# Matmul order in the projections and gate/up: each product runs over all token chunks in turn

## The reference, cut to what matters

```python
def hybrid_mixer(h, hc, ...):
    aq, ak, av, bq, bk, bv, z, xbc, dt = split_projection(h @ w_in)
    caq, cak, cav, cbq, cbk, cbv, cz, cxbc, cdt = split_projection(hc @ w_in)
    ...
    y = jnp.concatenate([out_a, out_b, out_c], -1) @ w_out

def swiglu(h, w_gu, w_down):
    gate, up = jnp.split(h @ w_gu, 2, axis=-1)
    return (jax.nn.silu(gate) * up) @ w_down
```

## Time and profile before

| what | us |
|---|---|
| median of 3 runs | 3884.65 |
| lowest and highest | 3880.82, 3886.8 |
| profiled execution, first to last instruction (span) | 3878.7 |
| PE busy in it | 3426.3 (88%) |
| DVE, POOL, ACT busy in it | 1871.5, 1411.6, 853.1 |

### The profile page before, as it was taken

How to read it: one execution, slowest core, us unless ns; L and a number is a source line. 1 busy time by engine, 2 the same in 40 slices (tenths; PEclk the granted TensorE clock), 3 DMA queues, 4 the chain that set the end, 5 groups by cost and what they waited for, 6 DMA issues and landing times. The chain is left out here.

```text
span 3878.7 us, 48787 instructions
## 1 busy us (share of the span) xinstructions
PE 3426.3 (88%) x17688; PEld 2858.7 (74%) x17688; DVE 1871.5 (48%) x2851; ACT 853.1 (22%) x1566; POOL 1411.6 (36%) x1019
## 2 busy tenths in 40 slices
PE   0969989877959999999996779999888789999997
PEld 0849988755838888888884549988656578888884
DVE  8977533687682222222228887534675522222125
ACT  1135432213050001000004126432211211010102
POOL 1343112243353333343334342103253444444443
PEclk9989999988979999999997879989978899999998
DMA  7500001002301111111102410001002011111111
GB/s 275 172 12 1 1 29 59 11 17 97 109 27 38 38 38 38 32 43 38 38 27 88 157 49 1 0 27 60 6 19 84 28 44 46 51 43 50 47 49 49
DMA packets 63853, 197.67 MB, mean 51 GB/s; under 512 B 6160, under 2 KB 16656, under 8 KB 62736
## 3 DMA queue, kind: packets, MB, share of 16 engines
q1 hardware_dynamic: 54736, 172.32, 13.5%
q10 hardware_dynamic: 9024, 24.14, 1.7%
HBM read 177.05 MB, written 19.40 MB: 51 GB/s over the span
## 5 line engine op out<-in xcount | busy, mean ns | idle before, releaser
L188 PE MATMUL ps<-h_hi,f_whi 128*128 128x512 f32 (+1 forms) x1760 | 652.0, 370 | 50.7 <-POOL h_lo L1911 25.2
L189 PE MATMUL ps<-h_lo,f_whi 128*128 128x512 f32 (+1 forms) x1760 | 651.1, 370 | 0.0
L190 PE MATMUL ps<-h_hi,f_wlo 128*128 128x512 f32 (+1 forms) x1760 | 650.3, 369 | 0.0
L2096 DVE TENSOR_TENSOR f_gated<-f_gated,ps 128x512 f32<-128x512 f32 (+1 forms) x110 | 69.8, 634 | 1006.9 <-PE ps L190 1006.9
L1993 POOL TENSOR_TENSOR f_whi<-f_wraw,small 128x1024 fp32r<-128x1024 f32 x128 | 242.7, 1896 | 569.4 <-PE ps L190 569.4
L2104 DVE SCALAR_TENSOR_TENSOR x_res<-ps,mod,x_res 128x512 f32<-128x512 f32 (+1 forms) x440 | 306.9, 698 | 242.1 <-PE ps L190 241.8
L188 PEld LDWEIGHTS ps<-h_hi,f_whi 128*128 128x128 f32 x1760 | 334.1, 190 | 109.5 <-issue 42.7
L190 PEld LDWEIGHTS ps<-h_hi,f_wlo 128*128 128x128 f32 x1760 | 333.6, 190 | 56.1
L189 PEld LDWEIGHTS ps<-h_lo,f_whi 128*128 128x128 f32 x1760 | 334.0, 190 | 55.5
L188 PE MATMUL ps<-f_ahi,f_whi 128*128 128x512 f32 (+1 forms) x880 | 328.3, 373 | 0.0
L189 PE MATMUL ps<-f_alo,f_whi 128*128 128x512 f32 (+1 forms) x880 | 323.5, 368 | 0.0
(11 more groups left out here) (218 smaller groups left out, 6484.3 us busy)
## 6 DMA issues: line engine op xcount, KB each, us to landing
f_wraw<-in_w_ffn SPq DMA_DIRECT2D x132, 512.0 KB, 3.6
ada_w<-in_w_ada SPq DMA_DIRECT2D x80, 512.0 KB, 4.0
wrawc<-in_w_in SPq DMA_DIRECT2D x26, 512.0 KB, 4.1
wrawab<-in_w_in SPq DMA_DIRECT2D x16, 512.0 KB, 4.5
wrawo<-in_w_out SPq DMA_DIRECT2D x16, 512.0 KB, 3.9
ada_w<-in_w_ada ACTq DMA_DIRECT2D x16, 512.0 KB, 4.3
x_res<-in_xT SPq DMA_DIRECT2D x8, 640.0 KB, 6.6
x_spill<-x_res ACTq DMA_DIRECT2D x8, 640.0 KB, 5.1
```

The lines of the kernel that those rows point to most:

```text
L188: pe.matmul(out, w_hi, h_hi, start=first, stop=False)
L189: pe.matmul(out, w_hi, h_lo, start=False, stop=False)
L190: return pe.matmul(out, w_lo, h_hi, start=False, stop=last)
L2096: dve.tensor_tensor(g, g, pl.bank(3 + c, tn), ALU.mult).then_inc(u_taken[c], 1)
```

## The change

The loop over chunks moves inside. For each contraction tile and each of the three products, the matmul is issued for chunk 2, chunk 0 and chunk 1 in turn, all with the same weights, before the next product follows. The set of matmuls, their shapes, operands and banks stay as they were, and each bank still sums in the same order. The waits for a chunk's input and its bank stand before that chunk's first matmul, which is now among the first three of a block. `full[c]` is still raised by the last matmul of the chunk, which is now among the last three. The down product, attention and all other engines' programs are unchanged, and so are the down product's calls of `three_pass`.

```diff
 def multiply_block(pl, pe, ring, at, chunks, full, taken, ready=None):
     pe.wait_ge(ring.ready, at.n + 3)
-    for c in ORDER:
-        if c in chunks:
-            t0, tn = CHUNKS[c]
-            for sem, count in ready[c] if ready is not None else ():
-                pe.wait_ge(sem, count)
-
-            pe.wait_ge(taken[c], at.number(c) + 1)
-            for k in range(KT):
-                mm = three_pass(pe, pl.bank(3 * at.par + c, tn), ring.hi[at.par][:, k, :],
-                                ring.lo[at.par][:, k, :], pl.hi[:, k, t0:t0 + tn],
-                                pl.lo[:, k, t0:t0 + tn], k == 0, k == KT - 1)
-            mm.then_inc(full[c], 1)
+    mine = [c for c in ORDER if c in chunks]
+    for k in range(KT):
+        hi, lo = ring.hi[at.par][:, k, :], ring.lo[at.par][:, k, :]
+        for w, h, start, stop in ((hi, pl.hi, k == 0, False), (hi, pl.lo, False, False),
+                                  (lo, pl.hi, False, k == KT - 1)):
+            for c in mine:
+                t0, tn = CHUNKS[c]
+                if start:
+                    for sem, count in ready[c] if ready is not None else ():
+                        pe.wait_ge(sem, count)
+                    pe.wait_ge(taken[c], at.number(c) + 1)
+                mm = pe.matmul(pl.bank(3 * at.par + c, tn), w, h[:, k, t0:t0 + tn], start=start, stop=stop)
+                if stop:
+                    mm.then_inc(full[c], 1)
```

More of the change, by code:

```diff
@@ L2026, in _ @@
                     pe.wait_ge(ready, i * 6 + (j + 3))
[L2027 to L2037, removed]
+                    for k in range(KT):
+                        for w, h, start, stop in ((hi, pl.hi, k == 0, False), (hi, pl.lo, False, False),
+                                                  (lo, pl.hi, False, k == KT - 1)):
+                            for c in chunks:
+                                t0, tn = CHUNKS[c]
+                                if start:
+                                    for sem, count in lead.ready[c]:
+                                        pe.wait_ge(sem, count)
+                                    pe.wait_ge((u_taken if up else g_taken)[c], i * 2 + (f + 1))
+                                mm = pe.matmul(pl.bank(3 * up + c, tn), w[:, k, :], h[:, k, t0:t0 + tn],
+                                               start=start, stop=stop)
+                                if stop:
+                                    mm.then_inc(gu_full[c], 1)
                 pe.wait_ge(ready, i * 6 + 8)
```

## The result

The changed kernel takes 4029.61 us (median of 4 runs, 4017.12 to 4033.61) where the kernel before takes 3884.37 (median of 4, 3880.82 to 3886.8): a ratio of 1.0365, with a 95% interval of 1.0351 to 1.0379, or +145 us. The forecast was 3989 with a range up to 4025. So the sign held and the waits that the forecast named came; the size did not, because the forecast put a term at nothing that costs 26 us, the change of width from one matmul to the next. The profiled execution took 4017.12 us, the shortest of the four, with a span of 4015.3, which is 136.6 more than in the earlier trace rows.

The account below looks back on a forecast made before the run. PE was taken as the bound, busy 3426 of 3878.7 us. Down-product waits 17.6 + 30, `project_ssd` 33, staggered starts 13, small ends 3 and clock 7 gave 104 us; added to 3884.65, this is 3989, range 3962 to 4025.

Parts of the forecast that it names:

- the sign: Whole kernel: the change makes it slower, at 94%, against 5% for faster and 1% for the same.
- the waits that the forecast named: Down product waiting for POOL, 11 times about 1.6 and 11 times about 2.5 us; `project_ssd` transposes waiting for ACT's Silu.
- a term at nothing: Distance between matmuls in the mixed order: unchanged at 0.23 and 0.12 us, so 0 taken, with 14 ns a possible gain.

Follow-up runs that it names:

- run 256: Not a follow-up run: in "widths run 256, 512, 512 in turn", "run" is a verb and the numbers are the columns of successive matmuls.

## What to carry to other kernels

Sums that run in parallel in several banks end at the same moment. Then the first consumer finds nothing ready that used to be ready a whole chunk earlier, so keep the staggered ends at least in the last block before a consumer; here that single block was worth 76 of 145 us. The Trainium skill, Perfetto Trace Analysis, section "Matmuls", advises to rotate independent groups through the banks so that one's evacuation overlaps the next one's matmuls; the runs agree, and add that the groups must end apart for it, which taking them in turn undoes. And read some rows past a border before calling its cost nothing.

## What the runs showed of the hardware

- Matmuls of one width are evenly spaced whatever the bank: 120 ns for 256 columns and 226 to 227 for 512 at the full clock. A change of width costs. Where widths run 256, 512, 512 in turn it is 233 ns from a 512 to a 256, 124 from a 256 to a 512 and 229 from a 512 to a 512, with three banks in turn as within one bank. Behind a single change from 256 to 512 the next five starts are 233, 236, 228, 233 and 231 ns apart, and behind the change back the first is 113.
- Shared weights in neighbouring matmuls save no weight load here (17688 in both) and no time.
- Behind pauses of 2.84 us in dense work the clock fell to the lower level for 3.4 us in 7 of 11 cases in five executions, in 9 and in 10 of 11 in two others; behind pauses of 2.38 us in 2 of 11, behind 1.81 us (first layer, 256 columns only) in 3 of 11, behind 1.58 us in none, and with matmuls in the pause in none.
- From POOL's end to the matmul that waits for it, it took 0.24 us where PE had stood still for 0.66 us or more, and 0.055 where matmuls had kept it at work until 0.25 or 0.41 us before. In the changed kernel this makes 4 us in 22 starts.
- Near its start, attention of the second layer ran 35 us at a clock of 0.51 in three of the thirteen profiled executions and at 0.97 in that of the kernel before, on unchanged code. This one stretch is worth 15 us, more than several of the terms above. With stages compared one by one such a difference is found; in the totals it is not.
